# Broadcasting sample queries by a DMA instead of by ones-matmuls, in a two-layer decoder step on eight cores

## The chip, the cores and the metric

The kernel runs on all 8 cores of one Trainium2 chip as a single launch, each core with its own share of the batch and no traffic between cores. The metric is the device time of one execution in microseconds, taken on the slowest core. The time before is 1620.26 us, the median of 3 runs (1619.46 to 1620.95).

## The reference

One inference step of a two-layer decoder is computed for two groups that share all weights: 8 prompt sequences of 2048 tokens, and 128 samples of one token each. A layer is

```
x += mixer(rmsnorm(x))                 # pooling (layer 0), gated short convolution (layer 1)
x += mem_attend(rmsnorm(x), k, v)      # cross-attention to 256 memory rows, 4 heads of 256
x += squared_relu_mlp(rmsnorm(x))
```

and the attention of one group is

```
q = einsum('btd,de->bte', u, w_q).reshape(b, t, 4, 256)
s = einsum('bthd,bnhd->bhtn', q, k) * 256**-0.5
o = einsum('bhtn,bnhd->bthd', softmax(s), v)
```

For the prompt group, k and v are computed from memory tokens. For the sample group they are read from a cache: per layer and sample 256 rows of 1024 fp32 values for k, and as many for v. A core gets one prompt sequence and 16 samples, thus 32 sample attentions in the two layers.

## The kernel before, in words

Activations stay on chip with the channels on the partitions (tile X, 8 chunks of 128 channels by 2064 tokens). A layer's tokens are cut into 5 tiles of 416 columns (the last one has 384 prompt tokens and the 16 samples). A matmul group is 8 matmuls that accumulate into one PSUM bank, mostly over 416 columns, about 1.4 us; the groups take the banks of PSUM in turn, 7 of them (`nxt`), and the eighth (`OBK`) gathers the sample outputs. Each engine works through its own queue in the order in which the program was written; a helper class follows which bytes are read and written and places the semaphore waits, those of a DMA's issue too. The order is written out by hand.

In `attn_phase(l)` the prompt attention alternates stages S(k) (scores of one tile, then `den`, which normalises them) and O(k-1) (output projection of the tile before, added to X on VectorE, DVE in the profile). The MLP follows: items of `stA` (up projection) and `stB` (down projection), 20 of each per layer. Between the groups small pieces are let in: the norms of later tiles (`norm_p`, which leaves a low part `lo` from DVE, and two groups later `norm_r`, a matmul that reads that `lo`), and the sample attentions, one to a stage. In O(k) the sample stands behind group 3 and `norm_p` and `norm_r` behind groups 4 and 6, for O(0) to O(2); in S(k) the sample stands behind group 5. Samples 0 to 6 (layer 0) or 0 to 7 (layer 1) lie in these stages, the others, `n_att` and up, in stA and stB.

Earlier, at the beginning of S(1), `QSAMP` projects the 16 sample queries into tile QS (16 partitions by 1024, bf16; ScalarE, ACT in the profile, copies them from PSUM). `sample(b)` then runs: `SB(b-1)`, eight small matmuls that weight the values of the sample before; `SDK(b+1)` and `SDV(b+1)`, the loads of the next keys (two of 512 KB on the SP queue) and values (on the POOL queue); and `SA(b)`, the scores. SA(b) makes query row b appear on all 128 partitions by two matmuls (a column of the identity, spread to 128 columns, by QS, 512 columns each) into two PSUM banks, and then eight `dot` instructions on DVE multiply a key tile (128 rows by 256) by the query and sum. `SE(b)`, the exponential, stands later on ACT. Key tiles are double-buffered, so a key load of sample b+1 waits for the dots of sample b-1.

Of the kernel before, what the change touches and what calls it, by code (L numbers as in the profile page):

```python
# [8 lines left out]
BF16 = mybir.dt.bfloat16  # L9
# [4 lines left out]
PE, ACT, DVE, POOL, SP = "pe", "act", "dve", "pool", "sp"  # L14
NCORES = 8
D = 1024
NCH = 8
SEQ = 2048
NS = 16
# [8 lines left out]
TW = 416  # L28
# [103 lines left out]
def build_program():  # L132
    nc = bass.Bass("TRN2", target_bir_lowering=False)
# [5 lines left out]
    def dout(name, shape):  # L139
        return nc.dram_tensor(name, list(shape), F32, kind="ExternalOutput").ap()  # L140
# [27 lines left out]
    nps_d = dout("nps", [NS, 15, D])  # L168
    ncs_d = dout("ncs", [NS, 2, D])

    memn_d = nc.dram_tensor("memn1", [128, NCH * NMEM], BF16, kind="Internal").ap()

    es = contextlib.ExitStack()
# [3 lines left out]
    def DV(ap):  # L177
        return V(ap, [])
# [53 lines left out]
    def sl(a, b):  # L232
        return slice(a, b)

    def PSv(bank, a, b, m=128):
        return V(PS[0:m, bank, a:b], [(PSB + bank * 2048, PSB + (bank + 1) * 2048)], excl=True)
# [11 lines left out]
    def nxt():  # L248
        b = bank_ctr[0] % bank_mod[0]
        bank_ctr[0] += 1  # L250
        return b
# [3 lines left out]
    def palloc(dt, shape):  # L255
        t = T(top[0], dt, shape)
        top[0] += (t.nbytes + 63) // 64 * 64
        return t

    X = palloc(F32, [NCH, NTOK])  # L260
    U3OFF = top[0]
# [4 lines left out]
    IDB = palloc(BF16, [128])  # L266
# [3 lines left out]
    SS = palloc(F32, [4, 8])  # L270
    PBZ = [palloc(BF16, [8, NS]) for _ in range(2)]
    QS = palloc(BF16, [D])
# [18 lines left out]
    def mm(out, lhsT, rhs, start, stop):  # L291
        P.add(PE, "c", lambda e, o=out.ap, l=lhsT.ap, r=rhs.ap: e.matmul(out=o, lhsT=l, rhs=r, start=start, stop=stop),  # L292
              [lhsT, rhs], [out])
# [9 lines left out]
    def dot(out, in0, in1, acc):  # L303
        P.add(DVE, "c", lambda e, o=out.ap, a=in0.ap, b=in1.ap, c=acc.ap: e.scalar_tensor_tensor(  # L304
            out=o, in0=a, scalar=1.0, in1=b, op0=ALU.mult, op1=ALU.mult, accum_out=c), [in0, in1], [acc])
# [35 lines left out]
    def cp(out, in_, eng=DVE):  # L341
        if eng == ACT:
            P.add(ACT, "c", lambda e, o=out.ap, i=in_.ap: e.copy(out=o, in_=i), [in_], [out])  # L343
        else:
            P.add(eng, "c", lambda e, o=out.ap, i=in_.ap: e.tensor_copy(out=o, in_=i), [in_], [out])  # L345
# [4 lines left out]
    def memset(out, val, eng=DVE):  # L350
        P.add(eng, "c", lambda e, o=out.ap: e.memset(o, val), [], [out])  # L351

    def dma(q, out, in_, chan, after=()):
        return P.add(q, "d", lambda e, o=out.ap, i=in_.ap: e.dma_start(out=o, in_=i), [in_], [out], chan=chan, after=after)  # L354
# [33 lines left out]
    def free(*names):  # L388
        for name in names:
            slot_free.append(slot_of.pop(name))  # L390
# [13 lines left out]
    def load_slowly(name):  # L404
        pieces.extend((name, kc) for kc in range(NCH))
# [8 lines left out]
    def W(name):  # L414
        return SLOT[slot_of[name]]
# [329 lines left out]
    RSTDE = T(U3OFF + U3_BYTES - TW * 4, F32, [TW])  # L745
# [194 lines left out]
    def attn_phase(l, fill=()):  # L940
        bank_ctr[0] = bank_ctr[0] % 8 % 7
        bank_mod[0] = 7
        su = Scratch(U3OFF)
# [4 lines left out]
        assert su.top <= RSTD.off  # L948
        WQK, VWO = W(f"wqk{l}"), W(f"vwo{l}")
        KSA = [T(WQK.off + i * 4096, F32, [D]) for i in range(4)]  # L950
        VSA = [T(VWO.off + i * 4160, BF16, [2, 4, 258]) for i in range(2)]
        WOS = T(WQK.off, BF16, [NCH, D])
        s2 = Scratch(SCRB)
# [8 lines left out]
        n_att = N_ATT_S[l]  # L962
        OBK = 7

        def stage(b):
            return (KSU, VSU, "u") if b < n_att else (KSA, VSA, "a")

# [9 lines left out]
        def QSAMP():  # L977
            Wq = W(f"wq{l}")
            npmt = TILES[NT - 1][2]
            for hf in range(2):  # L980
                bk = nxt()
                for kc in range(NCH):
                    mm(PSv(bk, 0, 512, m=NS), BT[1](kc, sl(npmt, npmt + NS)), Wq(kc, sl(hf * 512, (hf + 1) * 512)), kc == 0, kc == NCH - 1)
                cp(QS(sl(hf * 512, (hf + 1) * 512), p=(0, NS)), PSv(bk, 0, 512, m=NS), eng=ACT)
            free(f"wq{l}")
            load_slowly(f"up{l}_1" if l else "up0_0")

# [33 lines left out]
        def SDK(b):  # L1021
            KS, _, nm = stage(b)
            for x in range(2):
                i = (2 * b + x) % 4
                dma(SP, KS[i](), DV(ck_d[l, b, x * 128:(x + 1) * 128, :]), f"k{nm}{i}")

        def SDV(b):
            _, VS, nm = stage(b)
            v = VS[b % 2]
            for x in range(2):  # L1030
                memset(v(x, sl(0, 4), sl(256, 257)), 1.0, eng=POOL)
                dma(POOL, v(x, sl(0, 4), sl(0, 256)), DV(cv_d[l, b, x * 128:(x + 1) * 128, :].rearrange("p (h e) -> p h e", h=4)), f"v{nm}{b % 2}")

        def SA(b):
            KS, _, _ = stage(b)
            for h2 in range(2):
                bk = nxt()
                mm(PSv(bk, 0, 512), V(IDB.ap[0:NS, b:b + 1].broadcast_to([NS, 128]), IDB().ivs),
                   QS(sl(h2 * 512, (h2 + 1) * 512), p=(0, NS)), True, True)
                for x in range(2):  # L1040
                    for hh in range(2):
                        h = 2 * h2 + hh
                        kv = KS[(2 * b + x) % 4](sl(h * 256, (h + 1) * 256))
                        dot(kv, kv, PSv(bk, hh * 256, (hh + 1) * 256), SS(b % 4, sl(x * 4 + h, x * 4 + h + 1)))
            memset(PBZ[b % 2](), 0.0, eng=POOL)

        def SE(b):
# [2 lines left out]
        def SB(b):  # L1050
            _, VS, _ = stage(b)
            for x in range(2):
                for h in range(4):
                    mmx(V(PS[32 * h:32 * h + NS, OBK, 0:257], PSv(OBK, 0, 1).ivs, True), PBZ[b % 2](x * 4 + h),
                        VS[b % 2](x, h, sl(0, 257)), b == 0 and x == 0, b == NS - 1 and x == 1)

        def sample(b):
            last = n_att - 1 if b < n_att else NS - 1
            if b not in (0, n_att):
                SB(b - 1)  # L1060
            if b < last:
                SDK(b + 1)
                SDV(b + 1)
            SA(b)

        def fin_a():
# [97 lines left out]
        if l == 1:  # L1164
            SDK(0)
            SDV(0)
        def pre_of(b, first):
            return (lambda: SE(b - 1)) if b > first else None

        todo = [(pre_of(b, 0), lambda b=b: sample(b)) for b in range(n_att)]  # L1170
        todo.append((pre_of(n_att, 0), lambda: SB(n_att - 1)))

# [8 lines left out]
        for k in range(NT):  # L1181
# [28 lines left out]
            if k == 1:  # L1210
                QSAMP()
                if l == 0:
                    free("wv0")
                    load_slowly("dn0_0")
            S(k, mid_s)
            if l == 0 and k == 1:
                free("wo0")
                load_slowly("up0_1")
                SDK(0)
                SDV(0)  # L1220
# [35 lines left out]
        O(NT - 1, mid_o)  # L1256
        assert not todo and not pieces
        SDV(n_att)
        yield


        todo = [(pre_of(b, n_att), lambda b=b: sample(b)) for b in range(n_att, NS)]

        def last_k():
# [89 lines left out]
    for at in attn_phase(0, kv1_fill()):  # L1354
        if at == ("A", 16):
            conv["cin_c"] = load_u("cin_c", 0)
        if at == ("A", 18):
            conv["cin_h"] = load_u("cin_h", 1)
            load("cout")
            conv_nA(1)  # L1360
        if at == (3, 2):
            conv_nA(0)
        if at == ("A", 18):
            conv_nP(0)
        if at == (3, 3):
            conv_nB(0)
# [11 lines left out]
    for at in attn_phase(1, fill):  # L1378
        if at == (2, NT - 1):
            final_block = finish_phase()  # L1380
        elif at == (3, NT - 1):
            fill.append(lambda: final_block(done[0], done[0] + TAIL))
        elif at and at[0] == 3:
            ready(TILES[at[1]][0] + TILES[at[1]][1], final_block)
        elif at and at[0] == "T":
            t0 = TILES[NT - 1][0]
            assert done[0] == t0
            done[0] += TAIL
            ready(NTOK, final_block)
            done[0] = t0  # L1390
# [124 lines left out]
```

How the kernel before makes its waits and increments, by code:

```python
    def emit(name, e):  # L1403
        known = {}
        for op in P.q[name]:
            for d in op.cwaits:
                key = ("e", d.eng)
                if known.get(key, 0) < d.val:
                    e.wait_ge(sems[d.eng], d.val)
                    known[key] = d.val
            for ch, val in op.dwaits:
                key = ("c", ch)
                if known.get(key, 0) < val:
                    e.wait_ge(chans[ch], val)
                    known[key] = val
            ins = op.fn(e)
            if op.kind == "d":
                ins.then_inc(chans[op.chan], 16)
            elif op.sig:
                ins.then_inc(sems[name], 1)
        if name == SP:
            for ch, cnt in P.chan_count.items():
                if known.get(("c", ch), 0) < cnt * 16:
                    e.wait_ge(chans[ch], cnt * 16)
```

The softmax here doesn't subtract the row's maximum and nothing guards it: scores larger than these inputs give would overflow.

## Time and profile before

| | |
|---|---|
| median of 3 runs | 1620.26 us |
| profiled execution | 1619.59 us, of which the span of its slowest core is 1618.0 us |
| spans of the eight cores | 1610.3 to 1618.0 us, mean granted TensorE clock 0.991 to 0.996 |
| DMA traffic of the slowest core | 145.15 MB in 87190 packets |

The profile is of the slowest core. A busy share says how much of the span an engine had an instruction running; the chain of waits goes back from the last instruction to what released it, step by step. PE is TensorE, PEld its weight loads, SP the queue that issues the key loads. L292, L296 and L304 are the lines of the helpers `mm`, `mmx` and `dot`, so forms (shapes) tell one use of a helper from another.

### The profile page before, as it was taken

How to read it: one execution, taken by the hardware profiler on the slowest of the kernel's cores; microseconds unless marked ns; L12 is line 12 of the kernel's file. 1: busy time of each engine (PE TensorE's matmuls, PEld its weight loads, DVE VectorE, ACT ScalarE, POOL GpSimd, SP SyncE). 2: the span in 40 equal slices, each digit the busy share in tenths (PEclk: the TensorE clock that was granted, in tenths of full speed). 3: DMA queues.
4: the chain of work that ended last, by engine and by line, in shares of the span. 5: the costliest groups of instructions: out<-in, count | busy, mean ns of one | idle time of the engine just before them, and what ended most of it. 6: DMA issues, size and time to landing. Idle time of an engine off the chain costs nothing.

```text
span 1618.0 us, 28570 instructions; the slowest of 8 cores (1610.3 to 1618.0 us)
## 1 busy us (share of the span) xinstructions
PE 1562.5 (97%) x10218; PEld 901.6 (56%) x10218; DVE 864.4 (53%) x1924; ACT 567.3 (35%) x1071; POOL 113.8 (7%) x245
## 2 busy tenths in 40 slices
PE   4899999999999999999999998999999999999997
PEld 3775545555556655555555554555455655555565
DVE  5666775655443444445666665776565444442325
ACT  4756445541121221222133224543643112213453
POOL 2002121110000000000000001121010000000000
PEclk9899999999999999999999999999999999999999
DMA  8969793675537706066000009694555663000012
GB/s 225 208 113 165 163 177 71 127 144 83 85 65 131 123 1 105 10 96 110 1 1 1 1 1 168 116 202 103 120 118 73 98 105 53 14 1 1 40 65 107
DMA packets 87190, 145.15 MB, mean 90 GB/s; under 512 B 4350, under 2 KB 41470, under 8 KB 87036
## 3 DMA queue, kind: packets, MB, share of 16 engines
q0 software_dynamic: 67568, 84.08, 36.0%
q1 hardware_dynamic: 19484, 59.24, 11.1%
q8 instruction: 85, 1.39, 0.3%
q14 instruction: 53, 0.43, 0.1%
HBM read 212.42 MB, written 14.36 MB: 140 GB/s over the span
## 4 chain that ended last, share of the span: by engine, by line
PE 89%; DVE 4%; ACT 2%; issue 2%; DMA 2%; POOL 0%; DVEq 0%; ACTq 0%; SPq 0%; POOLq 0%
PE PS L292 85%; PE PS L296 3%; DVE MEM L327 3%; ACT MEM L319 2%; PE PS L301 1%; DMA MEM<-gv 1%; DMA MEM<-x 1%; DVE MEM L331 1%; ACT MEM L308 1%; DVE MEM L304 0%; DVE MEM L345 0%; POOL MEM L354 0%; DVEq L1409 0%; ACT MEM L343 0%; ACTq L1409 0%
## 5 line engine op out<-in xcount | busy, mean ns | idle before, releaser
L292 PE MATMUL PS<-MEM 128*128 128x416 bf16 (+7 forms) x8938 | 1477.5, 325 | 12.4 <-DVE MEM L331 5.3
L292 PEld LDWEIGHTS PS<-MEM 128*128 128x128 bf16 (+1 forms) x8938 | 828.7, 98 | 647.9 <-issue 54.8
L331 DVE TENSOR_TENSOR MEM<-PS,MEM 128x416 f32<-128x416 f32 (+6 forms) x558 | 312.2, 575 | 296.0 <-PE PS L292 260.7
L319 ACT ACTIVATE MEM<-PS 128x416 f32<-128x416 f32 (+5 forms) x469 | 238.7, 510 | 588.7 <-PE PS L292 578.6
L331 DVE TENSOR_TENSOR MEM<-MEM 128x416 bf16<-128x416 f32 (+3 forms) x282 | 160.4, 584 | 224.6 <-ACT MEM L319 205.3
L319 ACT ACTIVATE MEM<-MEM 128x416 bf16<-128x416 f32 (+9 forms) x299 | 184.9, 630 | 147.8 <-DVE MEM L331 112.8
L327 DVE SCALAR_TENSOR_TENSOR MEM<-MEM 128x416 bf16<-128x416 f32 (+7 forms) x322 | 177.0, 601 | 60.1 <-ACT MEM L319 50.2
L304 DVE SCALAR_TENSOR_TENSOR MEM<-MEM,PS 128x256 f32<-128x256 f32 x256 | 105.2, 420 | 60.1 <-PE PS L292 36.7
L296 PE MATMUL PS<-MEM 128*128 128x128 bf16 (+6 forms) x1096 | 75.2, 267 | 18.1 <-DVE MEM L339 7.3
L343 ACT COPY MEM<-PS 128x512 f32<-128x512 f32 (+3 forms) x73 | 39.1, 536 | 128.1 <-PE PS L292 111.8
L296 PEld LDWEIGHTS PS<-MEM 128*128 128x128 bf16 (+3 forms) x1096 | 52.9, 105 | 40.4 <-issue 39.3
L343 ACT CAST MEM<-PS 128x512 bf16<-128x512 f32 (+6 forms) x82 | 43.2, 531 | 90.5 <-PE PS L292 50.7
L319 ACT ACTIVATE PS<-PS 128x416 f32<-128x416 f32 (+2 forms) x67 | 33.2, 496 | 50.8 <-PE PS L292 50.8
L345 DVE CAST MEM<-PS 128x512 bf16<-128x512 f32 (+1 forms) x68 | 43.3, 656 | 12.5 <-PE PS L292 12.3
L354 POOL DMA_DIRECT2D MEM<-cv x64 | 47.7, 745 | 14.5 <-PE PS L292 14.2
L327 DVE SCALAR_TENSOR_TENSOR MEM<-PS,MEM 128x1024 f32<-128x1024 f32 (+1 forms) x17 | 21.8, 1283 | 44.5 <-ACT MEM L319 44.5
L301 PE MATMUL PS<-MEM 128*128 128x128 f32 (+5 forms) x184 | 25.0, 277 | 18.3 <-DMA MEM<-gv 8.4
L351 POOL MEMSET MEM<- 128x4 bf16 (+1 forms) x96 | 15.0, 159 | 352.4 <-PE PS L296 303.8
L301 PEld LDWEIGHTS PS<-MEM 128*128 128x128 f32 (+5 forms) x184 | 21.0, 147 | 21.2 <-issue 19.8
L339 DVE TENSOR_SCALAR MEM<-MEM 128x1024 bf16<-128x1024 f32 (+1 forms) x18 | 17.9, 997 | 23.3 <-ACT MEM L319 23.3
L354 POOL DMA_DIRECT2D MEM<-w_up x36 | 20.6, 582 | 134.1 <-PE PS L292 134.1
L354 POOL DMA_DIRECT2D MEM<-w_down x22 | 13.8, 636 | 207.2 <-PE PS L292 163.1
(28 smaller groups left out, 137.7 us busy)
## 6 DMA issues: line engine op xcount, KB each, us to landing
MEM<-ck SPq DMA_DIRECT2D x64, 512.0 KB, 6.1
MEM<-cv POOLq DMA_DIRECT2D x64, 256.0 KB, 6.1
MEM<-w_down POOLq DMA_DIRECT2D x6, 2048.0 KB, 18.0
MEM<-x SPq DMA_DIRECT2D x16, 512.0 KB, 13.1
MEM<-w_kv POOLq DMA_DIRECT2D x4, 2048.0 KB, 18.4
MEM<-w_o POOLq DMA_DIRECT2D x4, 2048.0 KB, 25.0
MEM<-w_up POOLq DMA_DIRECT2D x32, 256.0 KB, 12.7
MEM<-w_up POOLq DMA_DIRECT2D x4, 2048.0 KB, 18.0
```

Source lines behind the costliest of these rows:

```text
L292: P.add(PE, "c", lambda e, o=out.ap, l=lhsT.ap, r=rhs.ap: e.matmul(out=o, lhsT=l, rhs=r, start=start, stop=stop), [lhsT, rhs], [out])
L296: P.add(PE, "c", lambda e, o=out.ap, l=lhsT.ap, r=rhs.ap: e.matmul(out=o, lhsT=l, rhs=r, start=start, stop=stop, is_transpose=is_transpose ...
L301: P.add(PE, "c", lambda e, o=out.ap, i=in_.ap, d=ident.ap: e.transpose(out=o, in_=i, identity=d), [in_, ident], [out])
L304: P.add(DVE, "c", lambda e, o=out.ap, a=in0.ap, b=in1.ap, c=acc.ap: e.scalar_tensor_tensor(out=o, in0=a, scalar=1.0, in1=b, op0=ALU.mult, ...
L308: P.add(ACT, "c", lambda e, o=out.ap, i=in_.ap, a=acc.ap: e.activation(out=o, in_=i, func=AF.Square, accum_out=a), [in_], [out, acc])
L319: P.add(ACT, "c", lambda e, o=out.ap, i=in_.ap: e.activation(out=o, in_=i, func=func, bias=bias, scale=sc), rd, [out])
L327: P.add(eng, "c", lambda e, o=out.ap, a=in0.ap, b=in1.ap: e.scalar_tensor_tensor(out=o, in0=a, scalar=sc, in1=b, op0=op0, op1=op1), rd, [out])
L331: P.add(eng, "c", lambda e, o=out.ap, a=in0.ap, b=in1.ap: e.tensor_tensor(out=o, in0=a, in1=b, op=op), [in0, in1], [out])
L339: P.add(eng, "c", lambda e, o=out.ap, a=in0.ap: e.tensor_scalar(out=o, in0=a, scalar1=sc, scalar2=None, op0=op0), rd, [out])
L343: P.add(ACT, "c", lambda e, o=out.ap, i=in_.ap: e.copy(out=o, in_=i), [in_], [out])
L345: P.add(eng, "c", lambda e, o=out.ap, i=in_.ap: e.tensor_copy(out=o, in_=i), [in_], [out])
L354: return P.add(q, "d", lambda e, o=out.ap, i=in_.ap: e.dma_start(out=o, in_=i), [in_], [out], chan=chan, after=after)
```

## The change

The two matmuls of SA are taken out. After QSAMP the queries are stored once per layer to a tensor in DRAM (`q_d`), and for every sample a DMA on the SP queue (`SDQ`) reads row b of it with a stride of zero into all 128 partitions of a tile (2 KB on each). Two such tiles alternate: QBU[0], which is QS's own place, and QBU[1] for samples below n_att; for the others QBA[1], in a part of the VWO weights that is free after O(4). SDQ(0) follows the store in QSAMP, SDQ(n_att) follows O(4), every other SDQ(b+1) stands in sample(b) behind SDK(b+1) and SDV(b+1). Every SDQ waits for the store. The dots read the query from this tile (bf16) and not from PSUM (fp32), in the order of key halves, then heads.

```diff
+    q_d = nc.dram_tensor("qrows", [2, NS, D], BF16, kind="Internal").ap()
...
+        qst = []
+        QBU = [T(QS.off, BF16, [D]), T(U3OFF + 4 * 4096 + 2 * 4160 + 2 * TW * 4, BF16, [D])]
+        QBA = [QBU[0], T(VWO.off + 2 * 4160, BF16, [D])]
...
                 cp(QS(sl(hf * 512, (hf + 1) * 512), p=(0, NS)), PSv(bk, 0, 512, m=NS), eng=ACT)
+            qst.append(dma(SP, DV(q_d[l]), QS(p=(0, NS)), "qst"))
+            SDQ(0)
             free(f"wq{l}")
...
+        def SDQ(b):
+            dma(SP, (QBU if b < n_att else QBA)[b % 2](), DV(q_d[l, b:b + 1, :].broadcast_to([128, D])), f"qb{b % 2}", after=tuple(qst))
...
         def SA(b):
             KS, _, _ = stage(b)
-            for h2 in range(2):
-                bk = nxt()
-                mm(PSv(bk, 0, 512), V(IDB.ap[0:NS, b:b + 1].broadcast_to([NS, 128]), IDB().ivs),
-                   QS(sl(h2 * 512, (h2 + 1) * 512), p=(0, NS)), True, True)
-                for x in range(2):
-                    for hh in range(2):
-                        h = 2 * h2 + hh
-                        kv = KS[(2 * b + x) % 4](sl(h * 256, (h + 1) * 256))
-                        dot(kv, kv, PSv(bk, hh * 256, (hh + 1) * 256), SS(b % 4, sl(x * 4 + h, x * 4 + h + 1)))
+            qb = (QBU if b < n_att else QBA)[b % 2]
+            for x in range(2):
+                for h in range(4):
+                    kv = KS[(2 * b + x) % 4](sl(h * 256, (h + 1) * 256))
+                    dot(kv, kv, qb(sl(h * 256, (h + 1) * 256)), SS(b % 4, sl(x * 4 + h, x * 4 + h + 1)))
             memset(PBZ[b % 2](), 0.0, eng=POOL)
...
             if b < last:
                 SDK(b + 1)
                 SDV(b + 1)
+                SDQ(b + 1)
             SA(b)
...
         SDV(n_att)
+        SDQ(n_att)
         yield
```

## Rows read from the trace of the kernel before

**Rows 1.** The page: busy time by engine, and the chain by engine.

```profile
PE 1562.5 (97%) x10218; PEld 901.6 (56%) x10218; DVE 864.4 (53%) x1924; ACT 567.3 (35%) x1071; POOL 113.8 (7%) x245
...
PE 89%; DVE 4%; ACT 2%; issue 2%; DMA 2%; POOL 0%; DVEq 0%; ACTq 0%; SPq 0%; POOLq 0%
```

**Rows 2.** Windows, layer 0's samples: us, PE, PEld, DVE, ACT, POOL, clock, DMA share, GB/s.

```profile
150.00:380.00 230.00, 227.66 (x1405) 117.97 (x1403) 146.29 (x428) 103.35 (x184) 32.46 (x84) 1.00 0.67 130
```

**Rows 3.** Instruction groups by form, PE: count | busy us, mean ns | idle before.

```profile
L292 PE MATMUL PS<-MEM 128*128 128x416 bf16 x6248 | 1122.3, 339 | 6.1 <-DVE MEM L331 3.9 <-ACT MEM L319 1.6 <-DVE MEM L304 0.4
...
L292 PE MATMUL PS<-MEM 16*128 16x512 bf16 x64 | 19.2, 379 | 0.0
...
L292 PE MATMUL PS<-MEM 128*128 128x512 bf16 x64 | 16.6, 379 | 0.9 <-DVE MEM L345 0.9
```

**Rows 4.** Chain of waits around two SBs, in O(2) and O(4): start, us, what.

```profile
214.60 0.33 PE PS L296 x8
214.93 2.05 PE PS L292 x10
...
254.22 0.33 PE PS L296 x8
254.54 1.51 PE PS L292 x8
```

**Rows 5.** Timeline of DVE, layer 0's O(1): start, us, operation, [idle before].

```profile
187.40 0.56 DVE L331 TENSOR_TENSOR MEM<-PS,MEM 128x384 f32<-128x384 f32 x1 [0.27 <-PE PS L292]
188.11 0.42 DVE L304 SCALAR_TENSOR_TENSOR MEM<-MEM,PS 128x256 f32<-128x256 f32 x1 [0.15 <-PE PS L292]
```

**Rows 6.** Timeline of PE at the end of O(1).

```profile
193.32 0.66 PE L292 MATMUL PS<-MEM 128*128 128x416 bf16 x3 [0.42 <-DVE MEM L331]
```

**Rows 7.** Timeline of DVE, group 3 of O(2); S(1) of layer 1.

```profile
214.71 0.59 DVE L331 TENSOR_TENSOR MEM<-PS,MEM 128x416 f32<-128x416 f32 x1 [0.66 <-PE PS L292]
215.42 0.42 DVE L304 SCALAR_TENSOR_TENSOR MEM<-MEM,PS 128x256 f32<-128x256 f32 x1
...
1013.65 4.59 DVE L327 SCALAR_TENSOR_TENSOR MEM<-MEM 128x416 bf16<-128x416 f32 x8 [3.03 <-PE PS L292]
```

**Rows 8.** Instruction groups by form, DVE (columns as in Rows 3).

```profile
L304 DVE SCALAR_TENSOR_TENSOR MEM<-MEM,PS 128x256 f32<-128x256 f32 x256 | 105.2, 420 | 60.1 <-PE PS L292 36.7 <-DVE MEM L304 6.0
...
L327 DVE SCALAR_TENSOR_TENSOR MEM<-PS,MEM 128x1024 f32<-128x1024 f32 x16 | 20.5, 1284 | 43.0 <-ACT MEM L319 43.0
...
L327 DVE SCALAR_TENSOR_TENSOR MEM<-MEM 128x256 bf16<-128x256 f32 x8 | 3.3, 478 | 1.7 <-DMA MEM<-gv 1.7
...
L327 DVE SCALAR_TENSOR_TENSOR MEM<-MEM 32x1024 f32<-32x1024 f32 x1 | 1.3, 1284 | 0.0
```

**Rows 9.** Tile gv in the prelude (58.6) and the second MLP (1378.5): broadcast loads.

```profile
L354 SPq DMA_DIRECT2D MEM<-gv x1: 585/585/585, 58.6 to 58.6; - x1
DMA to landing us min/median/max: 18.4/18.4/18.4
...
L354 SPq DMA_DIRECT2D MEM<-gv x1: 328/328/328, 1378.5 to 1378.5; - x1
DMA to landing us min/median/max: 3.8/3.8/3.8
```

**Rows 10.** Timelines of SP, ACT and DVE, layer 1: keys, query copies, first dots.

```profile
1006.48 1.07 SPq L354 DMA_DIRECT2D MEM<-ck  x2
...
1007.58 1.03 ACT L343 CAST MEM<-PS 16x512 bf16<-16x512 f32 x2
...
1020.04 0.42 DVE L304 SCALAR_TENSOR_TENSOR MEM<-MEM,PS 128x256 f32<-128x256 f32 x1
```

**Rows 11.** DMA issues: out<-in, count, KB each, us to landing.

```profile
ys<-MEM SPq DMA_DIRECT2D x1, 64.0 KB, 1.9
```

**Rows 12.** Timelines of SP and DVE, layer 0's MLP: key loads; dots two samples later.

```profile
350.36 1.40 SPq L354 DMA_DIRECT2D MEM<-ck  x2
...
367.98 0.42 DVE L304 SCALAR_TENSOR_TENSOR MEM<-MEM,PS 128x256 f32<-128x256 f32 x1
```

More of the change, by code:

```diff
@@ L950, in attn_phase @@
         KSA = [T(WQK.off + i * 4096, F32, [D]) for i in range(4)]
+        qst = []
+        QBU = [T(QS.off, BF16, [D]), T(U3OFF + 4 * 4096 + 2 * 4160 + 2 * TW * 4, BF16, [D])]
+        assert QBU[1].off + QBU[1].nbytes <= RSTDE.off and su.top <= QBU[1].off
+        QBA = [QBU[0], T(VWO.off + 2 * 4160, BF16, [D])]
         VSA = [T(VWO.off + i * 4160, BF16, [2, 4, 258]) for i in range(2)]
```

## The prediction

> **What bounds the kernel now.** I read the page's totals and its chain first, then the time windows over the samples, the instruction groups by form, the chain piece by piece, and the timelines of VectorE (DVE) and of the queues. TensorE (PE) is busy for 97% of the span and carries 89% of the chain [rows 1]. The change acts where the sample attentions lie, and there it is tighter: from 150 to 380 us, which holds layer 0's samples, PE has 2.3 us of idle time in 230, at full granted clock (1.00, the 2.4 GHz level), while DVE is busy for 146 us, ScalarE (ACT) for 103, and the DMA engines for 0.67 of the time [rows 2]. So an instruction that leaves PE there shortens the run, unless another engine's queue is the next thing that PE waits for. Those places have to be found one by one.
>
> **What is removed.** 64 matmuls of 512 columns, two for each of 32 samples. As a group they are busy for 19.2 us, 0.30 us each [rows 3]; that counts the changeovers on both sides, of which one stays when SB's small matmuls meet the big ones directly. The chain has both cases with the same neighbours. In O(2), SB is followed by the pair and one group of 8 matmuls of 416 columns: 2.05 us. In O(4) only SB(6) is let in, so there the same group follows it without a pair: 1.51 us [rows 4]. The difference, 0.54 us, is a pair's price on PE. Bounds from both sides: 64 x 0.30 = 19.2 us above; below, by the 416-column matmul (1122.3 us / 6248 = 0.18 us, scaled to 512 columns 0.22), 64 x 0.22 = 14.1 us [rows 3]. I take 32 x 0.54 = 17.3 us, the row that has the very sequence.
>
> The Trainium skill ("TensorE: Matmul & The Clock Gate", Back-to-back issue gap) puts 518 cycles on an isolated gap of 512 columns, 0.216 us at the full clock. By it the pairs are worth an estimated 13.8 us; the rows have 0.30 us for these, because the changeover to and from a 16-row matmul is paid too, and I go by the rows.
>
> **Where PE then waits for DVE.** In O(0) to O(2) the order on DVE is: add of group 3, eight dots, add of group 4, the norm's `lo`; and two groups later PE's norm_r needs that `lo`. The dots of one sample take about 4 us (8 x 0.42 and gaps), so PE's margin there is about used up: at the end of O(1) it waits 0.42 us for DVE [rows 6]. What PE saves in front of norm_r then returns as waiting, except for what DVE itself can start earlier. Going through the six cycles, each with the savings at stake:
> - Layer 0, O(0): one pair (0.54). DVE has no idle time between group 3's add and `lo`. Lost: 0.54.
> - Layer 0, S(2) and O(1): two pairs (1.08). DVE idles 0.27 us before group 3's add and 0.15 before the dots, both for PE [rows 5]; these 0.42 can be won. Lost: 0.66.
> - Layer 0, S(3) and O(2): two pairs. Idle before group 3's add 0.66, between it and the dots (215.30 to 215.42) 0.12 [rows 7]: 0.78. Lost: 0.30.
> - Layer 1, S(1) and O(0): two pairs. From 1013.65 on, after the eight norm multiplies (4.59 us), DVE runs on practically without a gap, through two sets of dots [rows 7]. Lost: 1.0 of 1.08.
> - Layer 1's other two cycles as layer 0's: 0.66 and 0.30.
>
> Sum lost 3.5 us. The other 21 pairs (S(4), O(3) and all MLP samples) have no such `lo` behind the dots; their price is kept whole. Net 17.3 - 3.5 = 13.8 us.
>
> **The dots.** Only the place of the second input changes. No row has a dot with both inputs in SBUF. The nearest rows: the same instruction family with 1024 columns takes 1284 ns with an input in PSUM and 1284 with both in SBUF; a 256-column one in SBUF, with a per-partition scalar, takes 478 against 420 for the dot [rows 8]. Upper bound +58 ns, lower bound taken symmetrically at -58; I take 0, by the pair of rows that differ in nothing else. Where DVE has slack, either end costs nothing; in the six cycles (11 samples) 8 x 58 ns x 11 = 5.1 us hang on it. The waits of the dots for PE go; the wait for a DMA of the query comes.
>
> The Trainium skill ("VectorE: DVE Perf Modes", the errata section on SBUF sources) gives 58 fixed cycles for SBUF sources and 120 for PSUM, by which a dot would be an estimated 65 ns shorter. The 1024-column rows show no such difference. What it would do here is a rival below.
>
> **What is added.** Per layer one store of 32 KB, and 32 broadcasts in all that write 256 KB each: 8.4 MB on top of 145. The trace has such a broadcast, twice as wide (gv, one row to 128 partitions, 512 KB): 3.8 us to landing with the queues empty, 18.4 in the loaded prelude [rows 9]. I take 4 to 6 us, near the first, since the DMA share here is 0.67.
>
> *In the middle* the issue is early. SDQ(b+1) stands behind the two key loads of b+1, which wait for the dots of b-1 just as it does, so it adds no wait to SP that is not there. The shortest distance I find: keys issued 350.36 to 351.76, dots that use them at 367.98 [rows 12], leaving 16 us for the query. Hidden; the cover ends at 16 us.
>
> *At the start of a layer* SP waits for the ACT copies of QS, issues the store, waits for it, then issues SDQ(0); key loads stand behind. Layer 1 is the tight one: copies end at 1008.61, a store takes 1.9 us [rows 11], the broadcast 3.8: landing about 1014.5; the first dots come at 1020.04 [rows 10]. Margin 5.5 us. SDK(1), issued at 1006.48 before [rows 10], slips some 4.5 us and is needed one sample later. In layer 0, sample 0 comes only in O(0), so the margin is larger by a stage.
>
> *At n_att in layer 0* SDQ(7) waits for O(4)'s last group, as SDV(7) does on its queue, and SDK(8) stands behind it. The dots of sample 7 come four groups later, 32 x 0.18 = 5.8 us [rows 3], against 3.8. If it is late by a few us, DVE has only a copy to do there, and ACT does stA's squares; hidden.
>
> POOL's queue gets nothing new. PE's order is otherwise the same; two banks less per sample are taken from the seven.
>
> **Sum.** 1619.59 (the profiled execution, 1.6 us above its span) - 13.8 = 1605.8. The median shown is 0.67 above that execution, so against it I predict **1606.5 us**.
>
> **Rivals.**
> 1. *Pairs cheaper.* At the lower bound 14.1 us, the losses shrink too (about 2.4): gain 11.7, 1608.6. For it: PE could hide a changeover. Against it: the two pieces of the chain [rows 4].
> 2. *Dots faster in SBUF* by about 58 ns: 0.46 us per sample, which returns nearly all of the 3.5 lost: gain 17, 1603.3. Against it: the equal 1024-column rows [rows 8]. The errata rule named above would act so.
> 3. *Dots slower* by 58 ns: 13.8 - 5.1 = 8.7, 1611.6. For it: the 478 row.
> 4. *No change:* DVE or ACT takes over as the bound in the MLP samples too and every pair returns as waiting: 1619 to 1621. Against it: DVE is busy 146 of 230 us [rows 2].
> 5. *Slower: broadcasts later than their cover.* If every one took the prelude's 18.4 us, the dots would start 2.4 us late, DVE's queue would stop, and with two buffers each us of lateness is paid at every second sample, up to 16 times: 38 us, net 1606.5 + 38 = 1645. It decides from 16 us on; at 17 it eats the gain. For it: 128 reads of one 2 KB row, eight cores at once. Against it: 3.8 us for the wider one.
>
> That the change does not do what it says is not open: no other matmul broadcasts the query.
>
> **How the numbers follow.** Forecast (1602 to 1610) 0.66; rival 1: 0.07; rival 2: 0.10; rival 3: 0.08; rival 4: 0.04; rival 5: 0.05. From 1600 to 1611.5 lie the forecast, rivals 1 and 2 and nearly half of rival 3: over 8 in 10, some left out of the forecast's own edges. Below 0.2% (3.2 us) a run of this kernel cannot be told from no change. Faster by more: 0.66 + 0.07 + 0.10 + 0.08 = 0.91; within: 0.04; slower: 0.05.
>
> **What would show it.** The 16x512 form is gone and PE has 64 instructions fewer; behind SB, pieces of 1.51 us instead of 2.05; PE's waits for DVE in O(0) and O(1) grow to about 0.7 to 1.1 us; dots stay at 420 ns; the query loads land in 4 to 6 us and no dot waits for one. I am wrong if PE shows waits behind late dots in the MLP, if a DMA releases the dots, or if the pairs' time comes out near 0.43.

## The result, and the profile after

Run in turn on one chip, the changed kernel took 1608.26 us (median of 4 runs, 1606.59 to 1609.85) and the kernel before 1620.43 us: ratio 0.9925, 95% interval 0.9908 to 0.9943. The forecast was 1606.5 us. The profiled execution took 1608.05 us, with a span of 1606.3 us on its slowest core, now core 0. (In the later comparisons some executions had one die at a lower clock; all medians and ratios here leave them out.) The page of core 0, totals and chain by engine:

```profile
PE 1544.6 (96%) x10147; PEld 898.5 (56%) x10154; DVE 848.6 (53%) x1924; ACT 566.8 (35%) x1071; POOL 113.7 (7%) x245
...
PE 85%; DMA 6%; DVE 4%; ACT 2%; issue 2%; POOL 0%; DVEq 0%; ACTq 0%; POOLq 0%; SPq 0%
```

PE's busy time falls by 17.9 us against [rows 1] (on another core; in e0 it falls by 22.2, so this is not the price of the pairs), but the DMA's share of the chain rises from 2% to 6%: something that PE never waited for is now on the path. The windows over the samples of layer 0, which answer to [rows 2], and of layer 1:

```profile
150.00:380.00 230.00, 226.76 (x1421) 121.56 (x1421) 141.89 (x435) 104.30 (x186) 34.25 (x86) 1.00 0.81 154
1010.00:1240.00 230.00, 220.54 (x1372) 117.23 (x1371) 138.97 (x427) 101.64 (x181) 36.90 (x91) 0.99 0.75 142
```

In layer 0 little has changed but the DMA share (0.67 to 0.81). In layer 1 PE has 9.5 us of idle time, and its granted clock is below 1. The groups of PE and DVE, from the page ([rows 3, 8] before); the 16x512 form is gone:

```profile
L293 PE MATMUL PS<-MEM 128*128 128x416 bf16 (+6 forms) x8867 | 1459.9, 325 | 11.2 <-DVE MEM L332 4.3
...
L297 PE MATMUL PS<-MEM 128*128 128x128 bf16 (+6 forms) x1096 | 74.7, 267 | 26.5 <-DMA MEM<-cv 9.3
L305 DVE SCALAR_TENSOR_TENSOR MEM<-MEM 128x256 f32<-128x256 f32 x256 | 90.8, 420 | 4.6 <-DMA MEM<-qrows 4.6
```

PE (L297 holds SB) waits 9.3 us for `cv`, the sample values. A dot lasts 420 ns as before, yet the group is busy for 90.8 us instead of 105.2, so the dots overlap more than they did. The chain of waits on core 0, layer 1's samples ([rows 4] before):

```profile
1014.47 0.33 PE PS L297 x8
1014.80 1.51 PE PS L293 x8
...
1066.63 0.74 POOL MEM L355
1067.38 0.03 POOL MEM L352
1067.41 32.24 DMA MEM<-cv
1099.65 0.14 issue
1099.78 0.61 PE PS L297 x8
```

Behind SB stands the 1.51 us piece without a pair. Further on the path runs through a value load that takes 32.24 us from its issue. PE's timeline there, with the wait in brackets, shows that the load was wanted 6.76 us sooner, that is 25.6 us after its issue (1099.78 - 6.76 - 1067.41):

```profile
1082.98 0.40 PE L297 MATMUL PS<-MEM 128*16 128x257 bf16 x8 [1.05 <-DMA MEM<-cv]
...
1099.78 0.61 PE L297 MATMUL PS<-MEM 128*16 128x257 bf16 x8 [6.76 <-DMA MEM<-cv]
```

The whole run can be cut at the two starts of the query copies on ACT, of which the second is in [rows 10] for the kernel before. First its core 5, then cores 0 and 3 of the changed kernel (timelines of ACT):

```profile
135.12 1.03 ACT L343 CAST MEM<-PS 16x512 bf16<-16x512 f32 x2
```

```profile
131.86 1.03 ACT L344 CAST MEM<-PS 16x512 bf16<-16x512 f32 x2
...
996.00 1.03 ACT L344 CAST MEM<-PS 16x512 bf16<-16x512 f32 x2
```

```profile
131.19 1.03 ACT L344 CAST MEM<-PS 16x512 bf16<-16x512 f32 x2
...
993.71 1.03 ACT L344 CAST MEM<-PS 16x512 bf16<-16x512 f32 x2
```

The same from every core of every profile (us; start to first copies, from there to the second, from there to the end; the first has nothing of the change in it):

| kernel | start, mean (cores) | layer 0 | layer 1 | PE's waits for `cv`, sum of 8 cores |
|---|---|---|---|---|
| before | 131.2 (127.3-135.1) | 872.4-872.5 | 610.4-610.6 | 0 |
| changed | 131.1 (129.1-132.6) | 862.5-869.6 | 600.2-610.3 | 29.3 |
| e0, changed again | 131.3 (128.7-133.7) | 862.5-868.7 | 600.2-602.2 | 12.8 |
| e1, few broadcasts | 132.1 (128.6-134.2) | 862.2-865.1 | 600.2-600.5 | 5.6 |
| e2, before + broadcasts | 131.6 (127.9-135.0) | 872.4-872.5 | 610.3-610.5 | 0 |
| e4, pieces spread | 131.7 (127.7-133.7) | 862.4-865.3 | 600.2-600.4 | 3.3 |
| e5, pieces behind the sample | 132.2 (129.3-136.6) | 862.8-868.9 | 601.4-604.4 | 25.7 |
| e6, before, dots not held | 131.7 (129.6-134.8) | 871.0 | 609.0-609.1 | 0 |
| e7, MLP samples only | 131.9 (129.0-135.1) | 867.8-876.1 | 606.3-606.5 | 15.5 |
| e8, pairs put back | 134.1 (132.3-135.7) | 871.4-875.0 | 609.2-611.1 | 5.1 |

The last column holds the waits that the profile puts down to `cv`, and it misses some. At SB of sample `n_att` in layer 0, the first of the MLP stages, PE waits 0.96 us for ACT on every core of the kernel before too. On a few cores it waits longer there, still put down to ACT: 2.20 us on core 7 of e1, 2.28 on core 5 of e4, 2.90 on core 3 of e8. In each of the three the later of the sample's two value loads landed only 0.1 to 0.2 us before PE went on, so these are waits for values too. For core 3 of e8 this is 261.17 + 19.7 = 280.9 us (the wait, the load's issue, and its landing time):

```profile
281.01 0.40 PE L297 MATMUL PS<-MEM 128*16 128x257 bf16 x8 [2.90 <-ACT MEM L320]
...
261.17 0.74 POOL L355 DMA_DIRECT2D MEM<-cv  x1
...
DMA to landing us min/median/max: 19.7/19.7/19.7
```

Before, the two layers take the same time on all cores. After, the least disturbed cores gain 10.0 and 10.3 us, 20.3 in all, and the others give back up to 11.8 (core 0: 1.6 and 10.1). The slowest core decides: 1618.0 = 135.1 + 872.5 + 610.4 has become 1606.3 = 131.9 + 864.1 + 610.3.

### The profile page after: what moved, and what is told of

Read it like the earlier page. It is cut to its first block, busy times and chain, and to the rows that moved or that the text cites. A ratio compares the mean times of both kernels' runs of the same rounds, so it can differ in the third digit from the quotient of the medians.

```text
span 1606.3 us, 28266 instructions; the slowest of 8 cores (1592.7 to 1606.3 us)
## 1 busy us (share of the span) xinstructions
PE 1544.6 (96%) x10147; PEld 898.5 (56%) x10154; DVE 848.6 (53%) x1924; ACT 566.8 (35%) x1071; POOL 113.7 (7%) x245
## 4 chain that ended last, share of the span: by engine, by line
PE 85%; DMA 6%; DVE 4%; ACT 2%; issue 2%; POOL 0%; DVEq 0%; ACTq 0%; POOLq 0%; SPq 0%
PE PS L293 81%; DMA MEM<-cv 4%; PE PS L297 3%; DVE MEM L328 3%; ACT MEM L320 2%; PE PS L302 1%; DMA MEM<-gv 1%; DMA MEM<-x 1%; DVE MEM L332 1%; ACT MEM L309 1%; DVE MEM L346 0%; POOL MEM L355 0%; ACT MEM L344 0%; DVEq L1417 0%; ACTq L1417 0%
## 5 line engine op out<-in xcount | busy, mean ns | idle before, releaser
L293 PE MATMUL PS<-MEM 128*128 128x416 bf16 (+6 forms) x8867 | 1459.9, 325 | 11.2 <-DVE MEM L332 4.3
L332 DVE TENSOR_TENSOR MEM<-PS,MEM 128x416 f32<-128x416 f32 (+6 forms) x558 | 313.7, 576 | 355.4 <-PE PS L293 284.1
L332 DVE TENSOR_TENSOR MEM<-MEM 128x416 bf16<-128x416 f32 (+3 forms) x282 | 160.6, 584 | 226.9 <-ACT MEM L320 215.2
L297 PE MATMUL PS<-MEM 128*128 128x128 bf16 (+6 forms) x1096 | 74.7, 267 | 26.5 <-DMA MEM<-cv 9.3
L305 DVE SCALAR_TENSOR_TENSOR MEM<-MEM 128x256 f32<-128x256 f32 x256 | 90.8, 420 | 4.6 <-DMA MEM<-qrows 4.6
L297 PEld LDWEIGHTS PS<-MEM 128*128 128x128 bf16 (+3 forms) x1096 | 52.3, 105 | 49.0 <-issue 47.9
L355 POOL DMA_DIRECT2D MEM<-cv x64 | 47.6, 745 | 14.5 <-issue 10.1
L340 DVE TENSOR_SCALAR MEM<-MEM 128x1024 bf16<-128x1024 f32 (+1 forms) x18 | 17.9, 997 | 22.7 <-ACT MEM L320 22.6
L355 POOL DMA_DIRECT2D MEM<-w_down x22 | 13.8, 636 | 205.2 <-PE PS L293 163.1
## 6 DMA issues: line engine op xcount, KB each, us to landing
MEM<-qrows SPq DMA_DIRECT2D x32, 256.0 KB, 10.1
```

The lines of the kernel that those rows point to most:

```text
L332: P.add(eng, "c", lambda e, o=out.ap, a=in0.ap, b=in1.ap: e.tensor_tensor(out=o, in0=a, in1=b, op=op), [in0, in1], [out])
L340: P.add(eng, "c", lambda e, o=out.ap, a=in0.ap: e.tensor_scalar(out=o, in0=a, scalar1=sc, scalar2=None, op0=op0), rd, [out])
```

## The experiments

**e0: the changed kernel once more**, beside the next three on one chip.

> The changed kernel again, as the reference on this chip for the others. Both theories: about 1608 us against 1620, a ratio of 0.991 to 0.994; TensorE waits for late value loads (cv) on most cores, 0 to 9 us by core; the sum over the cores decides nothing, the slowest core does.

Measured: 1605.87 us (6 runs, 1601.56 to 1611.61), ratio 0.9919 (0.9902 to 0.9937). The spread of 10 us, against 3 for the kernel before, is a finding of its own: the waits for `cv` fall on other cores each time (0 to 4.6 us by core here, 0 to 9.3 in the first profile).

**e1: few broadcasts.** Only 4 of a layer's 16 are issued; the other samples read another sample's query row.

```diff
         def SDQ(b):
+            if b not in (0, 1, n_att, n_att + 1):
+                return
```

> The changed kernel with 4 of 16 broadcasts per layer left (samples 0, 1, n_att and n_att+1); the other samples read the query row that lies in the tile, so their scores are those of another query. Theory A (the broadcasts' DMA time makes the value loads late): no TensorE wait for cv, value loads land in about 6 us as before the change, and the time falls by the waits of the slowest core, to 1600 to 1603 us. Rival B (dots with both inputs in SBUF hold up the POOL queue, which issues the value loads): nothing changes in the waits, 1607 to 1609 us. Rival C (the value loads are late only because TensorE now asks for them earlier): waits for cv stay, most of them, 1605 to 1608 us.

Measured: 1600.63 us, ratio 0.9884 (0.9871 to 0.9897). With less traffic the waits for values shrink to at most 2.6 us on a core. So the broadcasts' traffic costs some 5 us of the run. Rival B falls: the dots still have both inputs in SBUF. The waits that are left all stand at `n_att` in layer 0; layer 1 has none.

**e2: the traffic alone.** The kernel before with all stores and broadcasts, into a tile that nobody reads; the pairs of matmuls stay.

```diff
+            qst.append(dma(SP, DV(q_d[l]), QS(p=(0, NS)), "qst"))
+            SDQ(0)
...
+        def SDQ(b):
+            dma(SP, QBX[0 if b < n_att else 1](), DV(q_d[l, b:b + 1, :].broadcast_to([128, D])), f"qb{b % 2}", after=tuple(qst))
...
                 SDV(b + 1)
+                SDQ(b + 1)
```

> The kernel before with its ones-matmuls, and beside them the 2 stores and 32 broadcasts of the change, into a tile that nobody reads. Theory A: the value loads get slower (9 us median instead of 6) and some come late; with TensorE about 5% slower in these stages than in the changed kernel the lateness is less, so 1620 to 1626 us, with waits for cv on some cores. Rival B: no wait for cv and 1620 us, since the dots read PSUM. Rival C: value loads land as late as in the changed kernel or not, but no wait, 1620 us.

Measured: ratio 1.0003 (0.9995 to 1.0012), and no wait for `cv` on any core. The same transfers cost nothing at the old pace and with the old dots, although they lengthen each other: values land after 6.6 to 9.5 us (median by core) instead of 5.2 to 6.3.

**e4: the weight pieces spread out.** While the stages run, `trickle()` sends a layer's next weights to the POOL queue in pieces of 256 KB, one at a call, 24 in the first calls of 36. Here every third call is passed over, so that they go out over all of the stages.

```diff
+    calls = [0]
...
     def trickle():
         if pieces:
+            calls[0] += 1
+            if calls[0] % 3 == 0:
+                return
```

> The changed kernel with the 24 weight pieces of each layer spread over all 36 places between O(0) and O(4) where a piece may be issued, by leaving out every third place, so that 8 pieces in the first two thirds come later. Theory A, with the value loads behind the weight pieces in a saturated DMA: cv waits shrink to below 2 us on the slowest core, 1601 to 1605 us. Rival B: the pieces do not matter, 1607 to 1609 us. Rival C: as A, less, 1604 to 1607 us.

Measured: 1601.42 us (1599.25 to 1602.07), ratio 0.9885 (0.9872 to 0.9899), the fastest version that computes everything. All broadcasts are in, and yet layer 1 is back at 600.2 to 600.4 on every core. What had cost the time there was the overlap of broadcasts and weight pieces, not the broadcasts. At `n_att` in layer 0 some lateness stays (1.35 and 1.92 us on cores 0 and 6, and the 2.28 of core 5).

**e5: the same pieces at other places**, in each stage behind the sample and not ahead of it.

```diff
-                    if ec % 2 == 0:
-                        trickle()
...
+                    if ec > 3:
+                        trickle()
```

(and in S at m = 5, 6 and twice at 7).

> The changed kernel with the weight pieces moved behind the sample of the same stage (in S behind groups 5, 6 and twice 7, in O behind groups 4 to 7), as many as before per stage: the values of a stage's sample are then issued ahead of that stage's pieces. Theory A1 (order: the value loads stand behind weight pieces in the POOL queue's rings): waits for cv below 2 us, 1601 to 1604 us. Theory A2 (amount: too many bytes between 1040 and 1100 us, in whatever order): the lateness remains in part, 1604 to 1608 us.

Measured: 1613.66 us, ratio 0.9939 (0.9910 to 0.9969). A miss: the waits for `cv` are as large as before the edit (25.7 us over the cores) and stand on every core. Issuing a stage's values ahead of that stage's pieces does not help; the pieces then stand bunched ahead of the next stage's values. Against e4, where the same pieces go out over a longer time, this speaks for the amount that is asked for at once. Whether the edit makes the kernel slower is not shown: the median is 8 us above e0's, but the intervals of the two ratios overlap, and the profile is of the fastest execution (1605.52 us).

**e6: the kernel before, with dots that don't wait for each other.** The helper class enters a read of PSUM as exclusive, so a dot waits for the dot before it on the same bank. This enters the dots' reads as shared.

```diff
-                        dot(kv, kv, PSv(bk, hh * 256, (hh + 1) * 256), SS(b % 4, sl(x * 4 + h, x * 4 + h + 1)))
+                        qv = PSv(bk, hh * 256, (hh + 1) * 256)
+                        dot(kv, kv, V(qv.ap, qv.ivs), SS(b % 4, sl(x * 4 + h, x * 4 + h + 1)))
```

> The kernel before, with one thing changed: the dots' reads of a PSUM bank are entered as shared reads, so that a dot no longer waits on a semaphore of the dot before it on the same bank (the matmuls that fill the bank still wait for them). Theory W (that wait, not the memory, spaces the dots 0.53 us apart): the dots follow each other at 0.35 us as they do in the changed kernel, eight take 2.8 us instead of 4, TensorE's waits for VectorE at the end of O(0) and O(1) go (0.2 and 0.4 us in each layer), and the time falls by 1 to 2 us, to 1618 to 1619. Rival M (a dot with an input in PSUM cannot overlap with the accumulator read before it): 0.53 us stays, 1620 us.

Measured: 1617.39 us, ratio 0.9976 (0.9958 to 0.9995), a little more than expected; layer 0 takes 871.0 us and layer 1 609.1 on all cores, 1.4 less each. The timelines of DVE, first the kernel before (the third dot waits for the second), then e6, then the changed kernel:

```profile
188.64 0.42 DVE L304 SCALAR_TENSOR_TENSOR MEM<-MEM,PS 128x256 f32<-128x256 f32 x1
188.99 0.08 DVE L304 DVE_READ_ACCUMULATOR MEM<-MEM,PS 128x1 f32 x1
189.24 0.42 DVE L304 SCALAR_TENSOR_TENSOR MEM<-MEM,PS 128x256 f32<-128x256 f32 x1 [0.17 <-DVE MEM L304]
...
192.12 1.98 DVE L331 TENSOR_TENSOR MEM<-PS,MEM 128x384 f32<-128x384 f32 x4
```

```profile
187.82 0.42 DVE L304 SCALAR_TENSOR_TENSOR MEM<-MEM,PS 128x256 f32<-128x256 f32 x1
188.16 0.08 DVE L304 DVE_READ_ACCUMULATOR MEM<-MEM,PS 128x1 f32 x1
188.16 0.42 DVE L304 SCALAR_TENSOR_TENSOR MEM<-MEM,PS 128x256 f32<-128x256 f32 x1
```

```profile
183.09 0.42 DVE L305 SCALAR_TENSOR_TENSOR MEM<-MEM 128x256 f32<-128x256 f32 x1
183.43 0.08 DVE L305 DVE_READ_ACCUMULATOR MEM<-MEM 128x1 f32 x1
183.43 0.42 DVE L305 SCALAR_TENSOR_TENSOR MEM<-MEM 128x256 f32<-128x256 f32 x1
...
185.85 1.52 DVE L332 TENSOR_TENSOR MEM<-PS,MEM 128x384 f32<-128x384 f32 x3
```

Where a dot waits for the one before it, the distance from dot to dot is 0.53 to 0.60 us; without the wait it is 0.34, wherever the query lies. In the changed kernel a sample's dots take 2.76 us (183.09 to 185.85); before, by the first dot of [rows 5] and the next add at 192.12, 4.01.

**e7: broadcasts for the MLP samples only**; those in the stages keep their pairs.

```diff
         def SDQ(b):
+            if not (b >= n_att):
+                return
```

> The changed kernel for the 17 samples of the MLP stages alone; the 15 samples of the S and O stages get their query by ones-matmuls as before. No broadcast runs beside the weight pieces. Theory A: no wait for cv; 17 pairs x 0.54 = 9.2 us gained, 1610 to 1611 us on every core. If the 15 stage pairs were worth nothing in the changed kernel, its 1606 to 1608 would be beaten; if they are worth 0.5 us each and the late values cost 5 to 9 us on the slowest core, the two kernels come out within 5 us of each other.

Measured: 1614.06 us, ratio 0.9958 (0.9939 to 0.9978), 4 us above what was expected. In the MLP of layer 0 nine pairs give 4.9 us as they should (351-us piece of the chain 244.6 us after the query copies before, 239.7 here, on core 1 of each), but 1.3 us of that is gone again by the next query copies (872.5 to 868.9 on most cores, 3.6). The trace shows where: at the end of layer 0 PE waits for DVE in one piece instead of two, and on cores 1, 3, 5 and 6 the next 75 matmuls take 14.65 us instead of 12.97 (14.33 on core 2), at a lower granted clock (0.64 from 970 to 974 us on core 1). On cores 0, 4 and 7, after the same wait, they take 12.97; why the clock fell on some cores only is open. Core 1 before, then here with the window:

```profile
968.99 2.75 PE L292 MATMUL PS<-MEM 128*128 128x416 bf16 x15 [2.24 <-DVE MEM L331]
972.87 12.97 PE L292 MATMUL PS<-MEM 128*128 128x400 bf16 x75 [1.13 <-DVE MEM L331]
```

```profile
969.19 14.65 PE L293 MATMUL PS<-MEM 128*128 128x400 bf16 x75 [3.10 <-DVE MEM L332]
...
970.00:974.00 4.00, 4.00 (x17) 1.90 (x16) 0.77 (x2) 0.00 (x0) 0.00 (x0) 0.64 1.13 208
```

And at `n_att` in layer 0, where the sample's loads can start only after O(4), PE waits 3.1, 5.9 and 3.9 us for `cv` on cores 0, 2 and 4. Cores 2 and 4 are the slowest of this run; core 2 takes 876.1 us for layer 0. The first profile of the changed kernel has no late value there, e0, e1, e4 and e8 have some; why they are later here is open. In layer 1, where nothing is late, the cores take 606.3 us against 600.2 on the undisturbed cores of the changed kernel, so the broadcasts of its 8 stage samples are worth 6.1 us there, pairs and dots together.

**e2b: distinct rows instead of broadcasts** in e2: 32 loads of 256 KB with 2 KB for each partition, of different addresses.

```diff
-            dma(SP, QBX[...](), DV(q_d[l, b:b + 1, :].broadcast_to([128, D])), ...)
+            dma(SP, QBX[...](), DV(x_d[b * 128:(b + 1) * 128, l * 512:(l + 1) * 512]), ...)
```

> The kernel before with 32 loads of 256 KB into an unread tile, as in the run with broadcasts beside it, but each of 128 different rows of 2 KB of x instead of one row 128 times. If reading one row 128 times is slow in itself, these loads land sooner than the 6.4 to 7.8 us (median by core) of the broadcasts, say in 4 to 5, and value loads in 6; if only the packets count, both are as there: 6.5 to 8, and values 6.6 to 9.5 us.

Measured once: 1621.32 us; these loads land after 5.9 to 7.1 us (median by core), the broadcasts of e2 after 6.4 to 7.8. Reading one row 128 times takes about as long as reading 128 rows. The values beside these loads land sooner than expected, after 5.8 to 7.2 us against 6.6 to 9.5 in e2; whether the broadcasts hold up other loads more, one execution of each does not settle.

**e8: the changed kernel with the pairs put back**, as matmuls into banks that nobody reads.

```diff
             qb = (QBU if b < n_att else QBA)[b % 2]
+            for h2 in range(2):
+                mm(PSv(nxt(), 0, 512), V(IDB.ap[0:NS, b:b + 1].broadcast_to([NS, 128]), IDB().ivs),
+                   V(IDB.ap[0:NS, b:b + 1].broadcast_to([NS, 512]), IDB().ivs), True, True)
```

> The changed kernel with a pair of ones-matmuls put back for every sample (64 matmuls of 512 columns, 16 rows, into PSUM banks that nobody reads); the dots go on reading the broadcast tile. Pace theory (the value loads come late only because TensorE runs 0.54 us per sample faster, so that the same traffic has less time): TensorE's waits for values are gone, as in the kernel before with the same transfers added, and the time is that of the kernel with the shared bank, 1617 us (ratio 0.9965 to 0.9985), spans of the cores within 8 us of each other. Rival (the early dots themselves, which let the next key loads start sooner and pack the transfers closer, make the values late): the waits for values stay at 3 us or more on several cores and the time is 1619 to 1622 (ratio 1.000).

Measured: 1621.45 us, ratio 1.0011 (0.9992 to 1.0031). The time lands where the rival put it, the named waits for `cv` nearer to the theory: at most 1.8 us on a core, 5.1 in all against 12.8 and 29.3. In layer 0's stages none is left (8.2 and 4.7 us in the two profiles of the changed kernel), but in layer 1's stages 5.1 us are (21.1 and 2.7), and at `n_att` in layer 0 PE waits 2.90 us on core 3, the slowest, and 1.8 to 2.2 on cores 0, 5 and 7, where 0.96 is usual. So neither theory holds alone, and how the lateness divides between the faster pace and the earlier dots this run does not decide. The parts of the run are cleaner than its time (the start was 2 to 3 us later in this profile than in the others): its least disturbed cores take 871.4 and 609.2 us. Core 1, whose span is 1613.5 us, is one (1004.28 - 132.86 and 1613.5 - 1004.28):

```profile
132.86 1.03 ACT L344 CAST MEM<-PS 16x512 bf16<-16x512 f32 x2
...
1004.28 1.03 ACT L344 CAST MEM<-PS 16x512 bf16<-16x512 f32 x2
```

## Why the prediction came out, and where it was wrong

The time is right, but of the sum only the pairs' price is; that the total comes out is luck. Two terms are wrong with opposite signs (by 5.9 us on DVE, by 11.8 us on late loads), and 3.2 us of the gain come from the start, in which nothing was changed. For the slowest core's span (-11.7 us; the forecast was -13.8):

| term | forecast | measured | from |
|---|---|---|---|
| pairs | -17.3 | -17.9 | e8 to undisturbed cores: 871.4 - 862.5 and 609.2 - 600.2 |
| DVE behind the dots | +3.5 | -2.4 | before to e8: 872.5 - 871.4 and 610.5 - 609.2 |
| late loads, core 0 | 0 | +11.8 | 864.1 - 862.5 and 610.3 - 600.2, plus rounding |
| start, core 5 to core 0 | 0 | -3.2 | 135.1 - 131.9 |

- **The pairs' price** (0.54 us each, from the chain) was right: 17.9 / 32 = 0.56. Rival 1 falls, and with it the estimate of 13.8 us from the issue gap of the Trainium skill alone.
- **"Where PE then waits for DVE" failed.** Its premise, "the dots of one sample take about 4 us (8 x 0.42 and gaps)", took the gaps for a property of the dots. They were waits of a dot for the dot before it (the gaps that [rows 5] leaves out). Without them DVE has 1.25 us per sample to spare, PE's waits for the adds of DVE (L332) shrink instead of growing (4.3 us against 5.3, slowest core of each; the two lines below, before and after). e6 shows it with nothing else changed: 2.9 us. The Trainium skill ("VectorE: DVE Perf Modes", The DRAIN you can't avoid) says of eight chained copies that a semaphore between them costs nothing extra. Here each such wait costs 0.19 us and more (0.53 to 0.34); the measurement decides.

```profile
PE PS L292 <- DVE MEM L331: 5.3, 9, 2.2
...
PE PS L293 <- DVE MEM L332: 4.3, 6, 1.9
```

- **The dots' duration** was right: 420 ns from either memory. Rivals 2 and 3 fall. The errata rule of the Trainium skill ("VectorE: DVE Perf Modes", the errata section on SBUF sources), by which a dot would be an estimated 65 ns shorter, does not show. Rival 2's gain of 17 us before late loads came nevertheless, and more, by another mechanism.
- **"They land in 4 to 6 us ... Hidden" failed**, in size for the broadcasts and in kind for the rest. The broadcasts land after 7.2 to 10.2 us (median by core), mostly still inside their cover; dots wait for a query in the first two MLP samples of layer 0 (1.0 and 3.6 us on core 0). That a DMA releases dots was one of the forecast's signs of being wrong; it also called such a lateness hidden, and on this core it was. But the forecast costed the 8.4 MB only by their own landing and went by "POOL's queue gets nothing new"; what else they delay was set to nothing. The mean DMA share of 0.67 hid the stretch that decides. Core 0 at the end of layer 1's stages, before (1053 to 1113 us) and after (1040 to 1100), busy tenths in 40 slices, queues, landing times:

```profile
DMA  9899999999944999999899999920000699999000
...
q0 software_dynamic: 5745, 4.85, 57.4%
q1 hardware_dynamic: 1667, 6.04, 27.5%
...
MEM<-cv POOLq DMA_DIRECT2D x8, 256.0 KB, 6.0
MEM<-w_up POOLq DMA_DIRECT2D x8, 256.0 KB, 10.1
```

```profile
DMA  9999999999999999999999999999999999999999
...
q0 software_dynamic: 5958, 5.41, 65.8%
q1 hardware_dynamic: 2248, 6.87, 42.4%
...
MEM<-cv POOLq DMA_DIRECT2D x8, 256.0 KB, 20.0
MEM<-w_up POOLq DMA_DIRECT2D x8, 256.0 KB, 24.1
MEM<-qrows SPq DMA_DIRECT2D x4, 256.0 KB, 13.4
```

Before, the engines caught up in a few slices; after, there is no free slice for 60 us, and the values on the *other* queue come after 20 us instead of 6. The Trainium skill ("DMA: Bandwidth & Descriptors", Issuing engines are not separate DMA queues) says that transfers from all queues run on the same 16 engines and interleave; the trace agrees, and by that sentence the values should have stood in my list. This is rival 5's mechanism (a transfer later than its cover), with another victim: not the query but the value, whose cover of 25.6 us was exceeded on some cores only. (On core 0 of e0 the same 60 us are as full and values land after 18.0 us, but PE waits for none.) e2 shows that the traffic alone is not enough, e1 that the pace alone costs little, e4 that thinning the weight pieces removes it from the stages, e5 that moving them behind the samples does not.

- **A late load costs more than its wait.** Core 0 waits 7.8 us for values in layer 1 but loses 10.1. The windows behind the long wait (the column before the last two is the granted clock):

```profile
1092.00:1100.00 8.00, 1.24 (x14) 0.51 (x12) 3.66 (x18) 3.10 (x2) 0.00 (x0) 0.84 1.06 222
1100.00:1104.00 4.00, 4.00 (x19) 1.64 (x12) 0.59 (x1) 0.00 (x0) 0.00 (x0) 0.50 0.72 169
1104.00:1108.00 4.00, 4.00 (x23) 2.20 (x22) 1.19 (x2) 0.00 (x0) 0.00 (x0) 0.96 0.06 8
```

After 6.8 us of idle time PE works for 4 us at 0.50, the 1.2 GHz level, and so loses 2 us more: 7.8 + 2, and 0.2 for the next window at 0.96, come near the 10.1.

Core 3 of e8 has the same: 1.9 us of wait beyond the usual 0.96 became 3.6 us (875.0 against 871.4).

Open: how much of the lateness is the pace and how much the earlier dots (e8 does not decide it), and why it strikes other cores in each execution.

## What to carry to other kernels

Before moving work from an engine to the DMA queues, look at the DMA share slice by slice over the stage, not at its mean, and list the loads of all queues with the cover of each: the one with the least cover pays, not the new one. Where transfers collide, spread the ones that are not urgent (here 1605.87 became 1601.42 us by that alone, e0 against e4). And when operations on one engine follow each other more slowly than their neighbours do, look for a wait between them before taking the gap for their cost.

## What the runs showed of the hardware

- A broadcast of one 2 KB row to 128 partitions (256 KB) lands about as fast as 128 distinct rows: 6.4 to 7.8 us against 5.9 to 7.1 beside the same traffic (e2 and e2b, one execution each).
- With the DMA engines full, a load of 256 KB went from 6.0 to 20.0 us (median of 8), one to 32.24, while the window's bytes rose only from 10.99 to 12.36 MB. With the pieces thinned (e4, core 0) the same 1040 to 1100 us hold 11.98 MB with hardly a free slice, and the values land after 11.3 us.
- The time to the first query copies differs from core to core by 3.4 to 7.8 us within one profile (127.3 to 135.1 us before), more than the smaller effects measured here; cutting the span at a fixed instruction takes it out.
